# Two transformer blocks on one core: sixteen more columns in the constants, 64 bytes further for every buffer behind them

## What is computed

```python
h = h + FFN_RESIDUAL_WEIGHT * g1 * rmsnorm(swiglu(y, ffn1_w_gate, ffn1_w_up, ffn1_w_down), ffn1_post_g)
h = h + g2 * rmsnorm(token_mix(y, w_in, conv_w, ...), mix_post_g)        # mLSTM and HGRN2
h = h + FFN_RESIDUAL_WEIGHT * g3 * rmsnorm(swiglu(y, ffn2_...), ffn2_post_g)
...                                                                     # then twice: mixer, MLP
```

## Time and profile before

| | |
|---|---|
| median of 3 runs | 2375.72 us (2374.66 to 2376.56) |
| the profiled execution | 2375.15 us, of which the span from the first to the last instruction is 2373.3 us |
| TensorE (PE) busy | 97% of the span, 11144 matmuls |
| weight loads (PEld) | 80%, under the matmuls |
| VectorE (DVE) / ScalarE (ACT) / GpSimd (POOL) | 56% / 36% / 9% |
| granted TensorE clock, mean | 0.989 |
| DMA | 287 MB, 121 GB/s on average |

### The profile page before, as it was taken

The page is one execution under the profiler, slowest core; times in us unless marked ns, Lnnn a source line. Parts: engine busy times, 40 slices in busy tenths (PEclk is TensorE's granted clock), DMA queues, the critical chain, the costliest instruction groups (busy, mean ns, idle before and its releaser), DMA issues.

```text
span 2373.3 us, 27594 instructions
## 1 busy us (share of the span) xinstructions
PE 2312.9 (97%) x11144; PEld 1906.5 (80%) x11144; DVE 1336.3 (56%) x1985; ACT 843.6 (36%) x1281; POOL 210.6 (9%) x177
## 2 busy tenths in 40 slices
PE   8999999999999999999999999999999989999998
PEld 6888887777787888888788988888977768888887
DVE  7655548495248465548543576664466664644343
ACT  3322224424334322223633342322344443423221
POOL 0000004021014000003110100000121101000001
PEclk8999999999999999999999999999999999999999
DMA  8766632311212366542231256664131111443331
GB/s 319 247 206 197 197 117 72 107 45 36 64 52 71 109 202 213 195 128 79 73 98 56 63 160 222 208 209 124 36 120 54 54 45 55 150 126 96 98 98 36
DMA packets 81918, 287.00 MB, mean 121 GB/s; under 512 B 9088, under 2 KB 11520, under 8 KB 81792
## 3 DMA queue, kind: packets, MB, share of 16 engines
q1 hardware_dynamic: 80928, 283.40, 37.4%
q10 hardware_dynamic: 864, 1.84, 0.2%
HBM read 283.10 MB, written 2.10 MB: 120 GB/s over the span
## 4 chain that ended last, share of the span: by engine, by line
PE 85%; DVE 9%; ACT 4%; issue 1%; POOL 0%; DMA 0%; DVEq 0%; SPq 0%; ACTq 0%; POOLq 0%
PE bank L284 23%; PE bank L286 23%; PE bank L285 23%; DVE wlo L1576 2%; PE bank L501 2%; PE bank L421 1%; PE bank L422 1%; PE bank L423 1%; PE bank L447 1%; PE bank L535 1%; PE bank L442 1%; ACT whi L987 1%; PE bank L443 1%; DVE attd L1956 1%; PE bank L334 1%
## 5 line engine op out<-in xcount | busy, mean ns | idle before, releaser
L1576 DVE TENSOR_TENSOR wlo<-raw,whi 128x1024 fp32r<-128x1024 f32 (+1 forms) x368 | 472.3, 1284 | 342.1 <-ACT whi L987 341.5
L284 PE MATMUL bank<-yhi,whi 128*128 128x512 f32 (+1 forms) x1670 | 655.7, 393 | 0.8 <-DVE ylo L1932 0.5
L286 PE MATMUL bank<-yhi,wlo 128*128 128x512 f32 (+1 forms) x1670 | 645.0, 386 | 0.0
L285 PE MATMUL bank<-ylo,whi 128*128 128x512 f32 (+1 forms) x1670 | 644.6, 386 | 0.0
L987 ACT ACTIVATE whi<-raw 128x1024 fp32r<-128x1024 f32 (+1 forms) x368 | 383.1, 1042 | 299.2 <-PE bank L286 250.6
L284 PEld LDWEIGHTS bank<-yhi,whi 128*128 128x128 f32 x1670 | 314.0, 188 | 81.0 <-issue 15.8
L286 PEld LDWEIGHTS bank<-yhi,wlo 128*128 128x128 f32 x1670 | 314.1, 188 | 64.7
L285 PEld LDWEIGHTS bank<-ylo,whi 128*128 128x128 f32 x1670 | 314.3, 188 | 61.4 <-issue 1.4
L284 PE MATMUL bank<-mlp_ahi,whi 128*128 128x512 f32 (+1 forms) x552 | 208.7, 378 | 0.0
L286 PE MATMUL bank<-mlp_ahi,wlo 128*128 128x512 f32 (+1 forms) x552 | 207.4, 376 | 0.0
L285 PE MATMUL bank<-mlp_alo,whi 128*128 128x512 f32 (+1 forms) x552 | 205.6, 372 | 0.0
(11 more groups left out here) (342 smaller groups left out, 2861.7 us busy)
## 6 DMA issues: line engine op xcount, KB each, us to landing
raw<-in_ada SPq DMA_DIRECT2D x152, 512.0 KB, 4.4
raw<-in_ffn_up SPq DMA_DIRECT2D x88, 512.0 KB, 4.4
raw<-in_mlp_up SPq DMA_DIRECT2D x64, 512.0 KB, 3.6
raw<-in_mlp_dn SPq DMA_DIRECT2D x64, 512.0 KB, 3.6
raw<-in_ffn_dn SPq DMA_DIRECT2D x32, 512.0 KB, 4.1
raw<-in_w_dqkv SPq DMA_DIRECT2D x24, 512.0 KB, 3.6
first<-in_ada SPq DMA_DIRECT2D x16, 512.0 KB, 14.9
raw<-in_ffn_dn SPq DMA_DIRECT2D x16, 384.0 KB, 3.5
```

The lines of the kernel that those rows point to most:

```text
L284: e.matmul(out, wh, xh, start=first, stop=False)
L285: e.matmul(out, wh, xl, start=False, stop=False)
L286: mm = e.matmul(out, wl, xh, start=False, stop=last)
L1576: e.tensor_tensor(k.wlo[:, what % NW, 0:width], raw[:, 0:width], k.f(k.whi[:, what % NW, 0:width]), ALU.subtract).then_inc(*sig.up("wlo", ...
```

## The change

The number of columns of the constants goes from 663 to 679. The array that the host fills gets 16 columns of zeros at its end, which no instruction reads, and the DMA that loads it moves 2716 instead of 2652 bytes for each partition.

```diff
-IDENT, ONES, PERM, CAUS, CNEG, INVF_C, EPS_C, HPI_C, SEL_C, QUAD_C, NCONST = 0, 128, 256, 384, 512, 640, 641, 642, 643, 647, 663
+IDENT, ONES, PERM, CAUS, CNEG, INVF_C, EPS_C, HPI_C, SEL_C, QUAD_C, NCONST = 0, 128, 256, 384, 512, 640, 641, 642, 643, 647, 679
```

## The result

The changed kernel takes 2391.24 us (median of 6 runs, 2388.27 to 2392.74) against 2375.75 us (6 runs, 2374.56 to 2380.05). The ratio is 1.0061, with a 95% interval of 1.005 to 1.0072: 0.6% slower, where I had forecast 0.2% faster and gave slower a chance of 0.06. The profiled execution of it is 2388.27 us, with a span of 2386.5 us, 13.2 us longer than that of the earlier trace rows.

What follows compares the result with a forecast made beforehand. TensorE was taken as the bound, busy 97% of the span. 2375.15 - 5.5 - 0.1 + 0.8 - 0.3 = 2370.05 us, stated as a 2370.5 us median (-0.22%), with an 8-in-10 range of 2368.8 to 2376.1.

Steps and rivals of the forecast that it cites:

- I take the start address modulo 128, not the stage, for the cause: Matmuls on hidden buffers, 64 bytes past a multiple of 128, step 2.2 ns slower because of that start address.
- the same four places: Runs behind the inference: yhi/ylo in "up" units, hidden activations in "down" units, weights as moving operand, and dxh/dxl.
- The clean cycle counts: Aligned paces of 544 cycles for 512 columns and 288 for 256, columns plus 32, taken as pointing to 128 bytes.
- the modulo-256 rival: Hidden buffers go from 64 to 128 bytes off the weights, 2.2 ns become 4.4: 2381.2 us; chance 0.06.
- Moving operands of 512 columns, 5.5 us gained: 2472 ffn and mlp "down" matmuls, all on the chain, go from 228.89 to 226.67 ns: 5.5 us gained.
- 256 columns, 0.8 us lost: 348 matmuls with moving operands of 256 columns, each 2.4 ns slower at the pace of yhi: 0.8 us lost.
- Seams, 0.3 us gained: Slow first nine "up" steps after a "down" unit go, 50 ns at each of 6 seams: 0.3 us gained.
- dxh, 0.1 us gained: Differential attention's output layer: 60 matmuls counted, each 2.2 ns faster, 0.1 us gained.
- VectorE, ScalarE, transfers: zero: Other engines' instruction times don't feel the address, and transfers cost or gain nothing on the chain: zero.
- The 16-byte rule: Lines are 16 bytes, so reads at 64 past a multiple of 128 begin cleanly: 2375.7 us; within a rival of chance 0.09.
- The clock, 1.7 us to either side: Stretches granted 1.2 GHz may fall on more or less work: taken as 0, with 1.7 us in the range.

Runs made afterwards that it cites:

- The table: Kernel without the network: blocks of 32 float32r matmuls of 512 columns, one per pair of weight and moving-operand starts; 226.8 ns a step at distance 0, 233.5 at 128 bytes.
- xb with wb: Block of that matmul-only kernel with moving operand and weights both starting 32 bytes past a multiple of 256; 7.44 us.
- 711 columns: Constants lengthened to 711 columns instead of 663 in the kernel before, putting the stage buffers at distance 0 from the weights modulo 256; 2375.32 us against 2377.12.
- 775 columns: Constants lengthened to 775 columns instead of 663 in the kernel before, stage buffers 256 bytes off the weights modulo 512; 2373.78 us against 2377.41.
- 743 columns: Constants of 743 columns, moving the stage buffers 256 bytes against the changed kernel, distance 128 modulo 256 again; pace 233.3 ns on ffn_ahi, as forecast.
- the two kernels with 128 unused bytes: Kernel before plus 128 unused bytes, either between ylo and raw (2405.07 us against 2377.12) or ahead of everything (2377.42 us, ratio 1.0004).
- 671: Constants of 671 columns, moving the stage buffers 32 bytes against the kernel before, to 96 past the weights modulo 256; pace 233.7 ns on ffn_ahi, as forecast.
- 727: Constants of 727 columns, moving the stage buffers 256 bytes against the kernel before, distance 64 modulo 256 again; pace 228.9 ns on ffn_ahi, as forecast.
- the matmuls alone: Kernel without the network, only back-to-back matmuls at varied distances, column counts and types; with 256 columns 4.05 us a block at 0, 3.87 at 192.

## Why the prediction was wrong

- *"I take the start address modulo 128, not the stage, for the cause"*: this is the step that failed. The stage was rightly excluded, but the address was not to be taken by itself. In every stretch at 226.7 ns that I had, the moving operand and the weights both lay at 128 past a multiple of 256; I read "both multiples of 128" where "the same residue" fitted the same four places. The two readings forecast opposite signs, and the case that tells them apart, an operand at 0 beside weights at 128, was in no row. The table shows 233.5 ns a step for it.
- *The clean cycle counts* (544 and 288, the columns plus 32) seemed to speak for 128 bytes and against the modulo-256 rival. They are real, but they belong to distance 0, and it is to be had at any residue (xb with wb, 7.44 us).
- *Moving operands of 512 columns, 5.5 us gained*: 11.0 us lost. The count, 2472, and their place on the chain were right, and so was the price of a nanosecond; the pace went from 228.9 to 233.3 and not to 226.7. At distance 0 (711 and 775 columns) the pace is the forecast one.
- *256 columns, 0.8 us lost*: 0.4 us lost, at 118.7 ns. At distance 0 they run at 120.0 ns, as forecast.
- *Seams, 0.3 us gained*: the nine steps after a "down" unit take 2.06 us in the changed kernel (232.48 to 234.54) where they took 2.09, at all six seams: 0.2 us gained. With 711 columns they take 2.04 (232.59 to 234.63), the whole of the forecast.
- *dxh, 0.1 us gained*: the same ten matmuls as in the earlier trace rows take 231.7 ns a step in the changed kernel (from 1976.29 us) where they took 228.9, so 60 x 2.8 ns = 0.2 us are lost. Even at distance 0 (711 columns) they take 230.9 and not 226.7 ns, since they follow a break.
- *VectorE, ScalarE, transfers: zero*: right. Line 1593 has 1218 ns on raw, with crow at a multiple of 128 now, and 1217 on first. The loads of the start did become faster, which the prediction had left open. The same stretch as in the earlier trace rows, in the changed kernel:

```profile
22.00:37.50 15.50, 15.50 (x66) 0.58 1.03 418
```

  418 GB/s against 408, and the chain from 15 to 57 us still holds no DMA. The same stretch has 418 with 743 columns too, where `first` is again at a multiple of 256, and 413 in the two kernels with 128 unused bytes, where `raw` begins at a multiple of 256 and `first` doesn't. It has 408 wherever neither does (671, 711, 727 and 775 columns). The Trainium skill (DMA: Bandwidth & Descriptors, How a descriptor splits into AXI transactions) says that a descriptor off a multiple of 256 bytes costs extra beats; by it, as an estimate, 4.5% of these loads. The trace agrees in sign, with 2.5% on a stream in which only a part of the loads moved. But the page speaks of bytes that are fetched, and here it was the destination that moved.
- *The rival "distance to the weights, modulo 256"* had the mechanism, the place and the deciding point ("above 228.9 ns"), and 0.06. It fitted the four places as well as the forecast did, and but for the clean cycle counts the rows gave no ground for 0.06 against 0.68. Its size was too small, 4.4 ns above the fast pace at 128 bytes where 6.7 were measured: 96 and 224 bytes cost as much as 128, so the cost isn't in proportion to the distance.
- *The 16-byte rule* (the Trainium skill: SBUF — State Buffer, Door 1: The DMA port swizzle), by which nothing should have changed, is not borne out for float32r: all starts here are multiples of 16 bytes, and the pace differs by 3%. For float32 and bfloat16 the runs agree with it.
- *The clock, 1.7 us to either side*: 1.5 us lost between the two profiled executions, of the right size. Of their 13.2 us, 11.4 are the paces, 1.5 the clock, 0.2 dxh, less 0.2 for the seams; 0.3 I can't place. The medians are 15.5 us apart, since the profiled execution of the changed kernel is the fastest of its six: it was granted 0.988, and the others, of 2388.8 to 2392.7 us, 0.984 to 0.987.

## What to carry to other kernels

Where TensorE is the bound and its operands are float32r with 512 columns in long unbroken stretches, lay moving operands and weights at the same start modulo 256 bytes: of the distances tried only 0 is free, 64 costs 1% and nearly all others 3% of the pace. With 256 or 448 columns another distance was faster, so measure there first. A buffer that grows by a few columns shifts everything allocated behind it, so look at the distances again after each such edit. And if a difference between two stages seems to come from an address, write down both operands' addresses before choosing a modulus: a cause that is inferred from cases in which two things never vary apart is a guess with two signs.

## What the runs showed of the hardware that I hadn't expected

- The pace of back-to-back float32r matmuls of 512 columns depends on the two operands' distance modulo 256 bytes: 226.7 ns at 0, 228.9 at 64, about 233 to 234 at 32, 96, 128, 160, 192 and 224, whatever the absolute start. It isn't symmetric: 64 ahead is cheap, 64 behind (192) is not. This holds where the starts stay the same from one matmul to the next.
- At 256 columns the order is another one: in the network 120.0 ns at 0, 117.6 at 64, 118.7 at 128; in the matmuls alone 192 is the fastest (3.87 us a block against 4.05 at 0).
- After a break the first nine steps at distance 0 take about 232 ns each (2.09 us on dxh with 711 columns) before the 226.7 ns set in.
- float32 (0.86 us a matmul, nearly four times as slow anyway) and bfloat16 (7.08 us for 32) don't show it at 512 columns.
- The mean duration of one line's matmuls can hide a change of pace: 394 and 395 ns on line 284, while the pace went from 228.9 to 233.3 ns. The distance of the starts shows it.
